# Two transformer blocks on one core: the order of ScalarE's copies and exponentials within an attention step

## What is computed

```python
# one_block(qb), inside nsa_mixer
s = einsum(q, k_cmp) - slopes * (t - cmp_center)            # compressed keys, 31 of them
o_cmp = (softmax(where(vis, s)) * vis) @ v_cmp
s = einsum(q, k_sel) - slopes * dist                        # selected blocks of keys
o_slc = softmax(where(dist >= 0, s)) @ v_sel
s = einsum(q, kw) - slopes * d                              # sliding window of keys
o_win = softmax(where(m, s)) @ vw
o = g0 * o_cmp + g1 * o_slc + g2 * o_win                    # gates from a sigmoid
```

## Time and profile before

| | before |
|---|---|
| median of three runs | 2241.24 us (2241.1 to 2243.33) |
| the profiled execution | 2240.84 us |
| its span, first to last instruction | 2238.9 us |
| PE busy | 2159.4 us, 96% |
| DVE busy | 1146.1 us, 51% |
| ACT busy | 746.6 us, 33% |
| POOL busy | 770.1 us, 34% |
| mean granted clock of TensorE | 0.981 |

### The profile page before, as it was taken

The page is one execution under the profiler, slowest core; times in us unless marked ns, Lnnn a source line. Parts: engine busy times, 40 slices in busy tenths (PEclk is TensorE's granted clock), DMA queues, the critical chain, the costliest instruction groups (busy, mean ns, idle before and its releaser), DMA issues.

```text
span 2238.9 us, 25526 instructions
## 1 busy us (share of the span) xinstructions
PE 2159.4 (96%) x9964; PEld 1704.7 (76%) x9964; DVE 1146.1 (51%) x1726; ACT 746.6 (33%) x1106; POOL 770.1 (34%) x198
## 2 busy tenths in 40 slices
PE   7999999999999888999999989999999998999999
PEld 6888888888888343788888867667678876888887
DVE  5445883672345777568548353566654745110121
ACT  4123221223313666332122244444453523321221
POOL 3444434443323210244344333221222233444433
PEclk9999999999999899999999989999999998999999
DMA  4223434422431000243333132111111122223322
GB/s 163 94 94 132 154 123 146 157 75 97 171 94 62 20 1 1 76 150 127 133 147 131 59 105 75 57 42 53 57 57 57 38 76 75 94 83 105 112 74 96
DMA packets 34202, 205.02 MB, mean 92 GB/s; under 512 B 4160, under 2 KB 5312, under 8 KB 14784
## 3 DMA queue, kind: packets, MB, share of 16 engines
q1 hardware_dynamic: 31968, 196.84, 25.0%
q10 hardware_dynamic: 2144, 6.95, 1.0%
HBM read 199.58 MB, written 2.10 MB: 90 GB/s over the span
## 4 chain that ended last, share of the span: by engine, by line
PE 89%; DVE 5%; ACT 3%; issue 1%; DMA 0%; POOL 0%; ACTq 0%; SPq 0%; DVEq 0%; POOLq 0%
PE PS L506 22%; PE PS L508 22%; PE PS L507 22%; PE PS L597 3%; PE PS L599 3%; PE PS L598 3%; PE PS L805 2%; PE PS L787 2%; PE PS L774 1%; PE PS L704 1%; ACT PB L1379 1%; PE PS L955 1%; ACT PT L1388 1%; PE PS L923 1%; DVE SPH L1620 1%
## 5 line engine op out<-in xcount | busy, mean ns | idle before, releaser
L444 POOL TENSOR_TENSOR WL<-WR,WH 128x2048 fp32r<-128x2048 f32 (+2 forms) x173 | 738.2, 4267 | 1345.2 <-ACT WH L1149 1345.2
L506 PE MATMUL PS<-Hh,WH 128*128 128x512 f32 x1536 | 606.3, 395 | 20.7 <-DVE Hl L1666 8.9
L507 PE MATMUL PS<-Hl,WH 128*128 128x512 f32 x1536 | 601.5, 392 | 0.0
L508 PE MATMUL PS<-Hh,WL 128*128 128x512 f32 x1536 | 601.0, 391 | 0.0
L1149 ACT ACTIVATE WH<-WR 128x2048 fp32r<-128x2048 f32 (+2 forms) x173 | 305.3, 1765 | 689.9 <-PE PS L508 637.7
L506 PEld LDWEIGHTS PS<-Hh,WH 128*128 128x128 f32 x1536 | 290.8, 189 | 87.4 <-issue 21.8
L507 PEld LDWEIGHTS PS<-Hl,WH 128*128 128x128 f32 x1536 | 290.8, 189 | 62.3 <-issue 2.2
L508 PEld LDWEIGHTS PS<-Hh,WL 128*128 128x128 f32 x1536 | 290.6, 189 | 61.3
L506 PE MATMUL PS<-Gh,WH 128*128 128x512 f32 x592 | 232.7, 393 | 0.0
L507 PE MATMUL PS<-Gl,WH 128*128 128x512 f32 x592 | 232.1, 392 | 0.0
L508 PE MATMUL PS<-Gh,WL 128*128 128x512 f32 x592 | 232.0, 392 | 0.0
(11 more groups left out here) (279 smaller groups left out, 2422.5 us busy)
## 6 DMA issues: line engine op xcount, KB each, us to landing
WR<-wA SPq DMA_DIRECT2D x125, 1024.0 KB, 4.8
AW<-wada SPq DMA_DIRECT2D x24, 1024.0 KB, 5.9
WR<-wB SPq DMA_DIRECT2D x24, 768.0 KB, 4.2
WR<-wC SPq DMA_DIRECT2D x24, 640.0 KB, 3.8
X<-x_in SPq DMA_DIRECT2D x8, 256.0 KB, 6.6
W1K<-w1k ACTq DMA_DIRECT2D x1, 2048.0 KB, 8.3
W1V<-w1v ACTq DMA_DIRECT2D x1, 2048.0 KB, 13.1
out<-X SPq DMA_DIRECT2D x8, 256.0 KB, 4.5
```

What stands on the lines that cost most here:

```text
L444: nc.gpsimd.tensor_tensor(WL[:, s, 0:n], WR[:, s, 0:n], WH[:, s, 0:n].bitcast(F32), ALU.subtract).then_inc(lo_s, 1)
L506: nc.tensor.matmul(PS[:, b, :], wh[:, c, cols], pe_h, start=c == 0, stop=False)
L507: nc.tensor.matmul(PS[:, b, :], wh[:, c, cols], pe_l, start=False, stop=False)
L508: last = nc.tensor.matmul(PS[:, b, :], wl[:, c, cols], pe_h, start=False, stop=c == seg.chunks - 1)
```

## The change

In each attention step ScalarE's four instructions come in another order: first the copies of both turned tiles, then both exponentials. The instructions themselves, their operands, their waits and their signals stay as they are, and so do the lists of the other engines.

```diff
             def attention():
+
+                def turned(m):
+                    _, _, qb, hf = tile_of(m)
+                    n = m // 8
+                    act.wait_ge(p_t, m + 1)
+                    if n >= 2:
+                        act.wait_ge(o_t, n - 1)
+                    nc.scalar.activation(PT[:, n % 2, hf, 0:qb + 1, qb * P:qb * P + P],
+                                         PS[:, (7, 3)[m % 2], 0:P * qb + P].rearrange("p (k q) -> p k q", q=P),
+                                         ACT.Copy).then_inc(p_s, 1)
+
+                def exponential(k):
+                    w = P * tile_of(k)[2] + P
+                    act.wait_ge(s_m, k + 1)
+                    nc.scalar.activation(PB[:, k % NPB, 0:w], PB[:, k % NPB, 0:w], ACT.Exp, scale=-1.0,
+                                         bias=NMX[:, k:k + 1], accum_out=SMX[:, k:k + 1]).then_inc(s_e, 1)
+
                 for p in range(NT // 2 + 4):
-                    for k in (2 * p, 2 * p + 1):
-                        if k < NT:
...
-                        m = k - 8
-                        if m >= 0:
...
+                    if p >= 4:
+                        turned(2 * p - 8)
+                        turned(2 * p - 7)
+                    if p < NT // 2:
+                        exponential(2 * p)
+                        exponential(2 * p + 1)
```

More of the change, by code:

```diff
@@ L1373, in attention @@
             def attention():
-                for p in range(NT // 2 + 4):
-                    for k in (2 * p, 2 * p + 1):
-                        if k < NT:
[L1377 to L1380, removed]
-                        m = k - 8
-                        if m >= 0:
[L1383 to L1390, removed]
+                def turned(m):
[12 more added lines that the diff above has]
+                                         bias=NMX[:, k:k + 1], accum_out=SMX[:, k:k + 1]).then_inc(s_e, 1)
+                for p in range(NT // 2 + 4):
+                    if p >= 4:
[4 more added lines that the diff above has]
+                        exponential(2 * p + 1)
             norm_root(EPS1)
```

## The result

The changed kernel takes 2210.17 us, the median of five runs (2207.5 to 2213.3); the kernel before, five runs beside it, 2242.29 us (2241.1 to 2247.11). The ratio is 0.986, 95% interval 0.9847 to 0.9872. The profiled execution is the slowest of the five, 2213.3 us, with a span of 2211.4 us.

A forecast was written before the change was run, and what follows sets the result against it. TensorE was taken as nearest to the bound, waiting for ScalarE's copies. Seven pairs 21.1 + start of attention 2.2 + clock 3.1 = 26.4 us off 2240.84 gives 2214.4, stated as 2215 us; range 2211 to 2223.

The forecast's parts named there:

- What bounds the kernel, and the unhindered unit: Attention: TensorE, nearest to full, waits for copies behind exponentials; unhindered 8.50 us a unit, 18.01 us a pair against 21.02.
- Both copies in time: Attention steps: with copies first, both are ready when TensorE needs them, the later one by 0.15 us.
- The exponentials' delay costs nothing: Attention: later exponentials are covered by the pipeline's depth, with 1.9 us in hand in the chain.
- ScalarE's wait for shifts: Sign expected in the profile: this wait, 55.6 us before, shrinks by as much as the attention stage does.
- The start of attention: Before the first value product: waits of the same cause and restart losses go, saving 2.2 us, between 1.2 and 3.5.
- The clock term: Two pairs of heads with stretches at 1.2 GHz lose them: 3.1 us saved, between 0 and 3.1.
- The last unit: Unit after the seven whole pairs of heads, at attention's end: has no exponentials and stays, so no saving counted.
- VectorE as bound: Rival (a), attention: VectorE takes over, up to 19.9 us a pair if GpSimd holds scalings; 2228, middle 2222 us; chance 0.13.
- the half gain: Rival (b), attention: ScalarE still not free in time, about half the loss stays; 2229 us; chance 0.05.
- the serial chain of depth two: Rival (c), attention: steps turn serial with only two steps of depth, 23.0 us a pair, 2255 us; chance 0.03.
- the four steps of depth: Attention pipeline: scores to scores four steps on take 6.6 us, against four steps of 8.50 to 9.51 us.
- the exclusive lock: Rule against the forecast: VectorE's two-port modes and GpSimd share ports, the later blocks fully; bias tiles could hold VectorE.

The follow-up runs named there:

- one-copy kernel: Changed kernel with ScalarE's order made copy, exponential, copy, exponential: 2222.52 us, ratio 0.9907 to the kernel before.
- exponentials-first kernel: Changed kernel with ScalarE's order made exponential, exponential, copy, copy: 2241.2 us, ratio 0.9996 to the kernel before.
- refilled kernel: Kernel before, with TensorE's waits for copies filled by repeated scores and turnings in width-128 steps from step 8 on: 2237.35 us, ratio 0.998.
- late kernel: Changed kernel with GpSimd's low part of wo's second weight unit moved behind the bias tiles and 126 shifts: 2210.42 us, on another chip 2215.8 us.
- the one with three more inverses: Changed kernel with VectorE's inverse of the row sums made four times in each step: 2228.44 us, 20.43 us a pair.

## Why the prediction was right and where it was wrong

- **What bounds the kernel, and the unhindered unit.** Right. I added 8.50 us a unit and 18.01 us a pair; every pair took 18.00. The loss was larger than the waits shown, as the sum by starts said.
- **Both copies in time.** Right: TensorE waits for a copy once, for 0.2 us, in seven pairs and a unit. The one-copy kernel shows what is lost when one of them is not in time (19.34 us, expected 19.3), the exponentials-first kernel that nothing else in the order counts.
- **The exponentials' delay costs nothing.** Right. The chain has room; VectorE's reserve is about 0.27 us a step. One sign was put wrongly: ScalarE's wait for shifts was to shrink by as much as the stage, 26.7 us, and shrank from 55.6 us to 4.4, since ScalarE now spends 27.3 us of its spare time waiting for turned tiles.
- **The start of attention.** 2.2 us forecast; 2.4 us between the two first profiles (21.52 to 19.14), and 2.5 between the means of three.
- **The clock term was the step that failed.** "There are two such pairs ... Their price is 2 x 1.53 = 3.1 us", and the bound "between 0 and 3.1". I took the count of one execution for the kernel's. In three profiles the pairs of heads lost 3.1, 6.2 and 4.4 us to low stretches, mean 4.6, and the last unit lost 0, 1.6 and 1.6 us (8.92, 10.50 and 10.50 us to `wo`), mean 1.1, which I had not counted at all: "The last unit after that has no exponentials and stays." Together 5.6 us, and the refilled kernel measures 5.7 by times. The changed kernel has none in three profiles. With 5.6 or 5.7 in place of 3.1 the sum is 21.1 + 2.2 + 5.6 = 28.9 us, and 2240.84 - 28.9 = 2212, inside the range and 2 us above the median measured. For the one execution that I had in front of me the forecast was nearly exact: 26.4 us, and the stage of the first changed profile is 26.7 us shorter. That execution's 2240.84 us was near the median by luck: it lost 2.9 to 4.7 us less to low stretches from the first value product on than the other two, but took 2 to 4 us longer from `wo` to the end. That it stood near the median did not mean that its low stretches were the usual ones.
- **The rest, 1 to 3 us.** The spans of the three profiles of each kernel differ by 29.9 us in the mean, the medians by 30 to 32. All 13 runs of the changed kernel have a median of 2210.56 us, 0.4 us below the range. The part before attention differs by 0.8 us in those means; both kernels' runs spread over 4 us or more by the clock elsewhere. I put the rest down to that spread; that is not shown, and no run shows a cause of its own.
- **The rivals.** VectorE as bound did not come, nor the half gain; the serial chain of depth two was out, as the four steps of depth said. GpSimd's long instruction held a scaling, 3.85 us before and 4.97 us in the late kernel, until about its own end. That fits the exclusive lock of the Trainium skill's page "SBUF — State Buffer", section "Who interferes with whom". The bias tiles hold scalings too, but for less. From GpSimd's and VectorE's timelines of the changed kernel, scalings under a pair of bias tiles and, in the last row, two of width 512 without any:

```profile
756.02 3.29 POOL L434 TENSOR_SCALAR BIAS<-DIST,slopes 128x512 f32<-128x512 f32 x2 [14.68 <-DVE NMX L1945]
...
756.04 1.27 DVE L1960 TENSOR_SCALAR PB<-PB,RMX,par 128x384 f32<-128x384 f32 x2
...
757.92 1.66 DVE L1960 TENSOR_SCALAR PB<-PB,RMX,par 128x512 f32<-128x512 f32 x2
...
857.42 1.00 DVE L1960 TENSOR_SCALAR PB<-PB,RMX,par 128x512 f32<-128x512 f32 x2
```

The two of width 384 take 1.27 us instead of 0.87, the two of width 512 1.66 instead of 1.00. That is 1.06 us a pair of heads, in both kernels alike, and not the 3.29 us of the rival. Both of width 384 are over at 757.31, while the first of GpSimd's two instructions runs until about 757.77 (its spans are rough), so for the bias tiles the trace does not agree with a full block. With all that, they cost TensorE nothing at 18.00 us a pair.

## What to carry to other kernels

On an engine that works through its list in order, put the instruction whose input is there and whose consumer is the bound first, and the one with a deep buffer behind it last; what is ready but stands behind a waiting instruction is paid by the engine that needs it. Size the gain by adding starts of unhindered pieces, not by the waits shown. Where the bound engine has short idle moments, look at several profiles for low-clock stretches before pricing them: one profile gives their price once, not on the mean. And move a long instruction of GpSimd only to where VectorE has no scaling to hold.

## What the runs showed that was not expected

Behind the start of attention TensorE fell to 1.2 GHz at two, four and three places in the three profiles of the kernel before, for 3.4 us each (once for 6.8 us in each of the last two). What stood ahead of the first value product or at the end of a unit there were two short waits, of 0.4 to 0.9 us; most units' ends had the same two waits and no low stretch. Work repeated in their place kept the clock at 2.4 GHz and made the kernel 4.5 us faster. The one-copy kernel (mostly one wait of 0.48 us a unit) and the one with three more inverses (1.85 us idle a pair) had no low stretch in seven pairs of one profile each, but both had one in the last unit. So idle moments of this size can bring a low stretch; which of them do is not shown.

And where the gap at the stage's start was filled with work, the 6.8 us at half clock there became 3.4 us in the first pair. Among the waits left ahead of that stretch were four of 0.76, 0.49, 0.53 and 0.19 us. Start and first pair together kept their length, 34.0 us against 33.6 and 33.7 in the two profiles of the late kernel.

The late kernel also shows the lesson of this change a second time: a copy that TensorE waited for 2.01 us stood behind two exponentials, which waited for a held VectorE.
